# Pair stage of an RWKV-7 and attention trunk: arrays with tokens on the partitions, halved by head or by chunk parity

## The reference

```python
def step(S, inp):
    r_t, w_t, k_t, v_t, a_t, b_t = inp
    sa = jnp.einsum('bhij,bhj->bhi', S, a_t)
    S = S * w_t[:, :, None, :] + sa[..., None] * b_t[:, :, None, :] + v_t[..., None] * k_t[:, :, None, :]
    return S, jnp.einsum('bhij,bhj->bhi', S, r_t)
y = (_wkv_scan(r4, dec4[0], kd4[0], v4, -kk, kk * a4[0], reverse=False)
     + _wkv_scan(r4, dec4[1], kd4[1], v4, -kk, kk * a4[1], reverse=True))
```

## Time and profile before

| | us |
|---|---|
| median of 3 runs | 1939.32 |
| lowest, highest | 1933.93, 1939.99 |
| the profiled execution | 1933.49 |
| its span | 1931.7 |
| PE busy | 1703.5 |
| DVE busy | 917.4 |
| ACT busy | 718.0 |
| POOL busy | 588.6 |

### The profile page before, as it was taken

How to read it: one execution, slowest core, us unless ns; L and a number is a source line. 1 busy time by engine, 2 the same in 40 slices (tenths; PEclk the granted TensorE clock), 3 DMA queues, 4 the chain that set the end, 5 groups by cost and what they waited for, 6 DMA issues and landing times.

```text
span 1931.7 us, 45633 instructions
## 1 busy us (share of the span) xinstructions
PE 1703.5 (88%) x20212; PEld 1339.5 (69%) x20212; DVE 917.4 (47%) x1151; ACT 718.0 (37%) x1118; POOL 588.6 (30%) x298
## 2 busy tenths in 40 slices
PE   4999768999999987879999999967878599999995
PEld 2777257888788885647777888735657388888884
DVE  3755655676666744263333430076662644444103
ACT  3422334444344422353343332243443444444221
POOL 0433032122212200423333444332102334444443
PEclk8999889999999998989999999978988799999997
DMA  7231000111111002435662232201111122333321
GB/s 307 88 128 35 27 7 8 47 53 31 31 51 49 27 5 68 153 145 204 238 240 86 87 120 90 73 11 55 43 45 55 33 87 87 98 96 105 105 75 44
DMA packets 43884, 161.13 MB, mean 83 GB/s; under 512 B 3664, under 2 KB 18256, under 8 KB 40912
## 3 DMA queue, kind: packets, MB, share of 16 engines
q1 hardware_dynamic: 43728, 158.75, 23.8%
HBM read 156.64 MB, written 2.10 MB: 82 GB/s over the span
## 4 chain that ended last, share of the span: by engine, by line
PE 82%; DVE 10%; ACT 4%; issue 3%; POOL 1%; DMA 1%; ACTq 0%; DVEq 0%; SPq 0%; POOLq 0%
PE ps L532 15%; PE ps L533 15%; PE ps L534 14%; PE ps L795 3%; PE ps L633 2%; PE ps L634 2%; PE ps L635 2%; PE ps L559 2%; PE ps L833 2%; DVE x_res L1573 2%; PE ps L787 1%; DVE area L1920 1%; PE ps L813 1%; PE ps L774 1%; DVE area L1503 1%
## 5 line engine op out<-in xcount | busy, mean ns | idle before, releaser
L1998 POOL TENSOR_TENSOR split_w<-raw_w,split_w 128x1024 fp32r<-128x1024 f32 (+1 forms) x148 | 380.7, 2573 | 743.7 <-ACT split_w L1140 743.7
L533 PE MATMUL ps<-h_lo_pad,split_w 128*128 128x512 f32 x800 | 321.3, 402 | 0.0
L532 PE MATMUL ps<-h_hi,split_w 128*128 128x512 f32 x704 | 283.3, 402 | 17.5 <-DVE h_lo_pad L1512 17.4
L1140 ACT ACTIVATE split_w<-raw_w 128x1024 fp32r<-128x1024 f32 (+1 forms) x148 | 167.2, 1130 | 353.9 <-PE ps L534 353.7
L534 PE MATMUL ps<-h_hi,split_w 128*128 128x512 f32 x704 | 279.6, 397 | 0.0
L532 PE MATMUL ps<-ff_hi,split_w 128*128 128x512 f32 x448 | 178.8, 399 | 8.3 <-DVE h_lo_pad L1512 8.3
L532 PEld LDWEIGHTS ps<-h_hi,split_w 128*128 128x128 f32 x704 | 133.8, 190 | 68.8 <-issue 29.1
L534 PE MATMUL ps<-ff_hi,split_w 128*128 128x512 f32 x448 | 175.8, 392 | 0.0
L533 PEld LDWEIGHTS ps<-h_lo_pad,split_w 128*128 128x128 f32 x800 | 152.0, 190 | 33.7 <-issue 0.5
L1587 DVE SCALAR_TENSOR_TENSOR ffs<-ffs,fcur 128x512 f32<-128x512 f32 x44 | 82.6, 1876 | 176.5 <-ACT ffs L1173 176.5
L1552 DVE TENSOR_TENSOR sx<-sx,ffs 128x512 f32<-128x512 f32 x32 | 22.2, 693 | 290.0 <-ACT ffs L1108 290.0
(11 more groups left out here) (267 smaller groups left out, 3361.4 us busy)
## 6 DMA issues: line engine op xcount, KB each, us to landing
raw_w<-in_ffn_up SPq DMA_DIRECT2D x88, 512.0 KB, 3.6
raw_w<-in_ffn_down SPq DMA_DIRECT2D x32, 704.0 KB, 4.1
late_a<-in_ada_w SPq DMA_DIRECT2D x7, 2048.0 KB, 8.4
late_b<-in_ada_w SPq DMA_DIRECT2D x7, 2048.0 KB, 10.1
o_res<-in_proj_w SPq DMA_DIRECT2D x24, 512.0 KB, 3.5
area<-in_ada_w SPq DMA_DIRECT2D x12, 1024.0 KB, 6.1
area<-in_ada_w SPq DMA_DIRECT2D x4, 2048.0 KB, 21.5
x_res<-in_xT SPq DMA_DIRECT2D x2, 2048.0 KB, 11.5
```

The lines of the kernel that those rows point to most:

```text
L532: mm(bank, wh[:, o:o + P], hi[:, t], start=(t == 0), stop=False)
L533: mm(bank, wh[:, o:o + P], lo[:, t], start=False, stop=False)
L1140: A(split_w[:, r % 2, 0, 0:cols], raw_w[:, r, 0:cols], ACT.Copy).then_inc(w_hi, 1)
L1998: G.tensor_tensor(split_w[:, r % 2, 1, 0:cols], raw_w[:, r, 0:cols], split_w[:, r % 2, 0, 0:cols].bitcast(F32), ALU.subtract).then_inc(w_l ...
```

## The change

Arrays with tokens on the partitions are now halved by the parity of the chunk: chunk c stands on half c mod 2, and head h takes another slot of columns, or another bank. Arrays with channels on the partitions stay halved by head. A product between channels and tokens therefore goes from half h to half c mod 2, over all four quarters: `system`, `grams`, `transposed`, `from_state`, `next_state`, and in `outputs` the values' and solutions' parts. A product from tokens to tokens (`from_values`, `solved`) or from channels to channels (the carry by the identity, the states' part of `outputs`) stays on two.

```diff
+        PAIRS = NCH // 2
+        split_heads = lambda ap: ap.rearrange("p n (c h) s -> p n c h s", h=2)
+        nt_h, gk_h, gb_h = split_heads(nt), split_heads(gk), split_heads(gb)
...
+            lanes = [(q, n, h) for q in range(NSEQ) for n in range(NDIR) for h in range(2)]
+            tiles_ = [(n, c, h) for n in range(NDIR) for c in range(NCH) for h in range(2)]
+            head = lambda h: slice(h * C, (h + 1) * C)
+            rows = lambda c: slice(c % 2 * C, (c % 2 + 1) * C)
+            slot = lambda c, h: c // 2 * 2 + h
+            cell = lambda n, c: slice((n * PAIRS + c // 2) * C, (n * PAIRS + c // 2 + 1) * C)
...
-            def lora_rates(r, banks=(1, 7)):
+            def lora_rates(r, banks=(6, 7)):
 
                 pe.wait_ge(keyed, r + 1)
+                if r > 2:
+                    pe.wait_ge(var_root, r - 2)
...
-                for n in range(NDIR):
-                    for c in range(NCH):
-                        for lo, hi in halves:
-                            last = mm(ps[lo:hi, 2 + n, c * C:(c + 1) * C], arn[q % 2][lo:hi, n, c, 0:C],
-                                      kbn[q % 2][lo:hi, n, c, C:P], start=True, stop=True)
-                    last.then_inc(sys, 1)
+                for n, c, h in tiles_:
+                    last = mm(ps[rows(c), 2 + h, cell(n, c)], arn[q % 2][head(h), n, c, 0:C], kbn[q % 2][head(h), n, c, C:P],
+                              start=True, stop=True)
+                last.then_inc(sys, 1)
...
+                pe.wait_ge(gram_in, 6 * q + 2)
+                for n, c, h in tiles_:
+                    last = mm(ps[rows(c), 4 + h, cell(n, c)], kbn[q % 2][head(h), n, c, C:P], arn[q % 2][head(h), n, c, C:P],
+                              start=True, stop=True)
...
+            def transposed(q, n):
+
+                if n == 0:
+                    for x in range(2):
+                        pe.wait_ge(tev[x], (LEVELS - 1) * (q + 1))
+                else:
+                    pe.wait_ge(gram_in, 6 * q + 6)
...
+            def transposed_values(q):
+
+                pe.wait_ge(gram_in, 6 * q + 4)
...
+            def carried(p, j):
+
+                pe.wait_ge(u_ev, CPS * p + j + 1)
+                last = from_values(p, j + 1)
+                if j > 0:
+                    for n in range(NDIR):
+                        for q in range(NSEQ):
+                            for h in range(2):
+                                last = mm(ps[head(h), n, s_col(q)], ident[head(h), head(h)], states[head(h), j, n, q, :],
+                                          start=False, stop=False, skip_group_check=True)
+                last.then_inc(carry_mm, 1)
+
+            def next_state(p, j):
+
+                pe.wait_ge(carry_mm, (CPS - 1) * p + j + 1)
+                for f in range(2):
+                    for q, n, h in lanes:
                         c = chunk(n, q, j)
+                        right = ut[rows(c), j, h, q, :] if f else vt[rows(c), slot(c, h), :]
+                        last = mm(ps[head(h), n, s_col(q)], kb[rows(c), n, f, slot(c, h), :], right, start=False, stop=(f == 1),
                                   skip_group_check=True)
                 last.then_inc(s_mm, 1)
...
+                last.then_inc(states_out, 1)
+                between()
+                pe.wait_ge(states_out, p + 1)
+                for n, c, h in tiles_:
+                    mm(ps[head(h), c % 2, cell(0, c)], vt[rows(c), slot(c, h), :], gk[rows(c), n, slot(c, h), C:P],
+                       start=False, stop=False, skip_group_check=True)
```

More of the change, by code:

```diff
@@ new lines, in grams @@
+                pe.wait_ge(gram_in, 6 * q + 2)
+                for n, c, h in tiles_:
+                    last = mm(ps[rows(c), 4 + h, cell(n, c)], kbn[q % 2][head(h), n, c, C:P], arn[q % 2][head(h), n, c, C:P],
+                              start=True, stop=True)
+                    if n == NDIR - 1 and c == NCH - 1:
+                        last.then_inc(gram, 1)
+            def transposed(q, n):
+                if n == 0:
+                    for x in range(2):
+                        pe.wait_ge(tev[x], (LEVELS - 1) * (q + 1))
+                else:
+                    pe.wait_ge(gram_in, 6 * q + 6)
+                for f in range(2):
+                    for c in range(NCH):
+                        for h in range(2):
+                            last = mm(ps[rows(c), (2, 4)[n] + h, cell(f, c)], kbn[q % 2][head(h), n, c, f * C:(f + 1) * C],
+                                      ident[head(h), head(h)], start=True, stop=True)
+                            if f == 1 and c == NCH - 1:
+                                last.then_inc(tr, 1)
@@ L843, in from_values @@
                 if j == 0:
                     last.then_inc(x0_mm, 1)
+                return last
             def from_state(p, j):
                 pe.wait_ge(s_ev, (CPS - 1) * p + j)
-                for n, q in lanes:
-                    for lo, hi in halves:
-                        last = mm(ps[lo:hi, 0, col(n, q)], arn[p % 2][lo:hi, n, chunk(n, q, j), 0:C],
-                                  states[lo:hi, j, n, q, :], start=False, stop=True, skip_group_check=True)
+                for q, n, h in lanes:
+                    c = chunk(n, q, j)
+                    last = mm(ps[rows(c), h, x_col(q)], arn[p % 2][head(h), n, c, 0:C], states[head(h), j, n, q, :],
+                              start=False, stop=True, skip_group_check=True)
@@ L874, in next_state @@
-            def next_state(p, j):
-                pe.wait_ge(u_ev, CPS * p + j + 1)
-                for n, q in lanes:
-                    for lo, hi in halves:
-                        last = mm(ps[lo:hi, 0, 256 + (2 * n + q) * C:256 + (2 * n + q + 1) * C],
-                                  kb[lo:hi, n, 1, chunk(n, q, j), :], ut[lo:hi, j, n, q, :], start=False, stop=True,
+                for q in range(NSEQ):
+                    for h in range(2):
+                        for n in range(NDIR):
+                            c = chunk(n, q, j)
+                            last = mm(ps[rows(c), h, u_col(q)], mf[rows(c), n, slot(c, h), :], x0s[rows(c), h, q, :],
+                                      start=True, stop=True)
@@ L882, in next_state, with outputs @@
                 last.then_inc(s_mm, 1)
-            def outputs(p):
+            def outputs(p, between):
                 pe.wait_ge(u_ev, CPS * (p + 1))
+                begun = set()
                 for j in range(1, CPS):
-                    for n, q in lanes:
+                    for q, n, h in lanes:
                         c = chunk(n, q, j)
-                        for lo, hi in halves:
-                            last = mm(ps[lo:hi, 0, c * C:(c + 1) * C], states[lo:hi, j, n, q, :], arn[p % 2][lo:hi, n, c, C:P],
-                                      start=(j == 1 and n == q == 0), stop=False, skip_group_check=True)
+                        last = mm(ps[head(h), c % 2, cell(0, c)], states[head(h), j, n, q, :], arn[p % 2][head(h), n, c, C:P],
+                                  start=(c % 2, h) not in begun, stop=False, skip_group_check=True)
+                        begun.add((c % 2, h))
@@ L899, in outputs @@
                 for j in range(CPS):
-                    for n, q in lanes:
+                    for q, n, h in lanes:
                         c = chunk(n, q, j)
-                        for lo, hi in halves:
-                            last = mm(ps[lo:hi, 0, c * C:(c + 1) * C], ut[lo:hi, j, n, q, :], gb[lo:hi, n, c, :], start=False,
-                                      stop=True, skip_group_check=True)
+                        last = mm(ps[head(h), c % 2, cell(0, c)], ut[rows(c), j, h, q, :], gb[rows(c), n, slot(c, h), :],
+                                  start=False, stop=True, skip_group_check=True)
@@ L970, in stage @@
                         if scans:
+                            carried(p, 1)
                             next_state(p, 1)
@@ L1276, in sigmoid, with rates @@
                 A(dst, ps[:, bank, :], ACT.Sigmoid, bias=pc(col)).then_inc(evac, 1)
-            def rates(r, banks=(1, 7), first=0):
+            def rates(r, banks=(6, 7), first=0):
                 act.wait_ge(pcols, r + 1)
@@ L1284, in rates, with decays @@
                     sigmoid(4 * r + first + n + 1, t_a[n], banks[n], 2 + n)
-            def decays(r, banks=(1, 7), first=2):
+            def decays(r, banks=(6, 7), first=2):
                 act.wait_ge(pcols, r + 1)
```

173 lines of the change are left out of this document (82 added, 91 removed).

## The result

The changed kernel takes 1949.36 us (median of 8 runs, 1944.4 to 1954.33), the kernel before beside it 1937.28 (8 runs, 1933.54 to 1939.99). The ratio is 1.0065, with a 95% interval of 1.0049 to 1.0082. The forecast was 1903, with a range to 1927. The profiled execution took 1946.96 us.

A forecast was written before the change was run, and what follows sets the result against it. PE's order of work was taken to bound the pair stage. Savings by stage, 3.5 + 4 + 5 x 4.8 + 4 + 1 = 36.5 us, took the median from 1939.3 to 1903 us, range 1881 to 1927.

The forecast's parts named there:

- idle by "issue" at zero: PE's idle time by "issue" was left unchanged, at zero, with −5 to +15 us allowed.
- the modulation load at nothing: The 1 MB modulation load, issued 4 us earlier and wanted 1 us sooner after its first product, was to cost nothing.
- Rate of four quarters: 64x64 products on PE were to go from 29.2 to 14.6 ns per record, despite the new bank pattern.
- the rival that ended at 1951: Quarters don't overlap in the new bank pattern: 29.2 ns per record in all 560 records a stage, slower, 1951 us; 7%.
- The ceiling of 10.0 us a stage: Most that PE could save in a full stage: 8.2 us on 64-column records and 1.8 on 128-column grams.
- Step 1: Stage start to first factors: PE waits 2 us for both evictions and POOL; the point comes 0.1 us later.
- Step 2: Levels: at level 1 PE waits 1.1 us for DVE's masks, plus 0.25 us for `carried` before `next_state`.
- Steps 3 and 4: Level 3 waits for DVE till 32.9 to 33.9 (PE there at 33.1); in outputs, modulation waits 0.5 us for DVE's bonus product.
- Step 5: Grams: DVE's six evictions, some 0.62 us each, set the pace to 51.5; next `system` at 54.0 instead of 59.06.
- Clock: Rival: holes in PE's work pull the granted clock to 0.92, costing 14 us, so 1917 us; 9%.
- the supply at 13%: Rival: instruction supply eats half the gain, mean 22 ns per record, 20 us saved, 1919 us; 13%.

The follow-up runs named there:

- m1_supply: Separate kernel of 64x64 products alone, written out or looped, not a variant of either kernel; four quarters took 27.0 ns per record written out, 17.3 looped.
- e2: Changed kernel with systems made by direction again, DVE evicting direction 0 first so POOL starts earlier, four quarters kept; 1934.39 us, ratio 0.9970.
- e10: Changed kernel with systems by direction, direction 0 evicted first, plus one unused filler product ahead of PE's wait for POOL; 1927.66 us, ratio 0.9946.
- e17: Kernel before, with POOL starting only after both directions' evictions and doing its second operation twice; 1962.87 us, ratio 1.0113.
- e1: Changed kernel with two unused filler products before PE's wait for POOL in each pair's first factors; 1941.82 us, ratio 1.0020.
- e14: Kernel before, with POOL and DVE's own next operation waiting until both directions' systems are evicted; 1948.56 us, ratio 1.0047.

## Why the prediction was wrong

It got the array right and the stage wrong. The steps that failed are idle by "issue" at zero, the modulation load at nothing, and a sum that had the hole before the first factors without the clock behind it. Waits of PE in the stage at 369.75, which had the full clock (us in total, times, longest):

```profile
PE ps L769 <- POOL area L2098: 2.4, 1, 2.4
PE ps L804 <- DVE area L1877: 1.2, 2, 1.0
PE ps L812 <- issue: 1.2, 2, 0.9
PE ps L826 <- issue: 1.1, 1, 1.1
PE ps L791 <- issue: 0.9, 1, 0.9
PE ps L867 <- issue: 0.7, 1, 0.7
PE ps L832 <- DVE area L1927: 0.5, 1, 0.5
```

All its waits sum to 8.8 us, 4.5 of them "issue"; before, the stage of the earlier trace rows had 1.1, all of it "issue".

- *Rate of four quarters.* Right within short runs: `system` takes 1.24 us in this stage, and in three of the six its 64 records start within 0.94 us, 14.9 ns apart. The new bank pattern doesn't matter (m1_supply), so the rival that ended at 1951 has no part in this; that the time came near its price is chance. The ceiling of 10.0 us a stage was too high as busy time: 7.5 in this stage. That the rest is the drain of each group, which every new wait lays open, is argued, not shown.
- *Step 1.* The forecast was a wait of 2 us. It is 2.4 here and 2.6 on average, as POOL's first operation is 0.5 longer than its row of before. The mechanism is right; but I counted only its length. Behind it the lower clock level held for 27.3 us, up to 13.7 us of loss, beside the 15.5 us of waiting. Undoing the late eviction gave back 15 us (e2).
- *Step 2.* Right: 1.1 forecast, 1.0 to 1.2 us measured in each of the six stages. The wait for `carried` isn't to be seen in any row.
- *Steps 3 and 4.* No row shows a wait for DVE at the fourth level (0 to 0.8 forecast). The wait for the bonus product, 0.5, didn't come.
- *Step 5.* DVE was to set the pace of the grams. It accounts for 0.5 us here; in the other stages PE stands at the grams for instructions, up to 3.86 us at a time.
- *Modulation load at nothing.* I asked only whether its data would be late, and they weren't. But in the changed kernel 11.7 of the 30.6 us of "issue" are gaps whose instruction packet began while such a load was on its way, against 2.7 us before. That moving the loads would give this back isn't shown.
- *Issue at zero.* This term failed. Its row, 16.4 us before L787, is of weight loads (PEld), which run ahead of PE; PE's own idle by "issue" was 13.9 us, with none before L787. It went from 13.9 to 30.6 us in six stages, 16.7 more, just over the +15 that I gave for the whole. I took 14.6 ns from a run of 1 us and carried it over a stage of 1888 records. By m1_supply's 27 ns, an estimate for this code, 1888 records need some 51 us whatever the array does, and the forecast stage of 54.0 left nearly nothing for the times in which a block comes late. Where such records follow one another for long, straight code can have 2.2 of the 14.6 ns that were to be saved on each.
- *Clock.* I had it as a rival of its own, 14 us at 9%, and the supply at 13% with 20 us left. They aren't alternatives: both act in the same stages and add up, and 20.4 of the 47.8 us at the lower level begin at gaps in the supply. Over six stages: busy time −30.0 (with the low clock in it), POOL +15.2, issue +16.7, DVE +9.7, ACT +1.3; sum 12.9 of the 13.4 us. The forecast had these stages 28 us shorter, so it missed by 41; "issue" is 16.7 of that, and the clock at most 23.9.

So the answer to where the gain went: less array time turned into waits for instructions, which cost clock too, and the later eviction opened a hole that costs itself and the clock. Undoing the second part alone makes the change a gain of 0.3%, and with the filler 0.5% (e10). The first part isn't mended here.

## What to carry to other kernels

A rate read from a run of 1 us is not that of a stage: before a change that makes small instructions shorter, compare the count of instructions with what long straight code was ever supplied at (here 27 ns for a product with its load), and keep such code in a loop where it can be one (shown for products alone, not tried in the kernel). Look also at which large transfers are on their way when the next instructions have to come. When an engine at the bound gets a hole of 2 us, count the clock behind it as well as the hole; an event that another engine needs early should be signalled as soon as its half is there, and a useless product can be cheaper than idling.

## What the hardware showed that was not expected

- Straight code: 128 products with loads per 3.45 us, after a first run of 271 without a stop; the same in a loop 17.3 ns each, with one gap of 0.11 us.
- Two halves of 128 rows by 64 columns don't overlap in fp32: 54.5 ns for 128 moving columns, as much as one after the other; quarters of 64x64 do, at 14.6 to 16.3 ns.
- In e17, 1.10 us of work in 2.90 us was followed by a stretch at 1.2 GHz; two filler products in each such hole are worth 7 us over the kernel (e1 against the changed kernel).
- An instruction packet that falls into a 1 MB load begins late: 23 of 24 gaps of more than 2 us follow packets 4.9 to 7.0 us apart, against 3.2 us at the least.
- Of two elementwise operations on 128x512 that DVE and POOL start within 0.04 us of each other, the second is longer: POOL 1.77 in place of 1.27 us behind DVE (after), DVE 1.79 in place of 0.69 behind POOL (e14), in all six stages of each.
